# Two products of the third projection placed together behind the first products of each level

## The chip, the cores and the metric

The kernel runs on one core of one Trainium2 chip. The metric is the device time in microseconds (us) of one execution; the median of the runs shown counts.

## The reference, cut to what matters

Two transformer blocks over 512 tokens of width 1024. The change lies in the second block, in its RWKV-7 mixer. Sixteen heads of 64 columns each keep a 64x64 state that is updated token by token:

```python
def step(state, inp):
    r_t, w_t, k_t, v_t, a_t, b_t = inp
    sa = jnp.einsum('bhij,bhj->bhi', state, a_t)
    state = state * w_t[:, :, None, :] + sa[..., None] * b_t[:, :, None, :] + v_t[..., None] * k_t[:, :, None, :]
    return state, jnp.einsum('bhij,bhj->bhi', state, r_t)
```

The inputs r, k and v of a pair of heads are three projections of the normed tokens, `proj = n @ w_in`, 128 columns each. The dilated attention beside it reads projections of the same tokens.

## The kernel before, in words

The kernel is one program with the engines' instruction streams written out by hand: each engine has its own block of code, and they meet only through counted semaphores. `p_pe.step("p10")` on an instruction means that it raises TensorE's counter when it is done; `pe.wait_ge(p_dve.sem, p_dve.done("z10", at))` holds TensorE's stream until VectorE has done the step of that name.

**The mixer's passes.** The RWKV heads are worked on in eight passes, one pair of heads each. `pair_pass` stands once in each engine's block (TensorE line 1752, ScalarE 2545, VectorE 3307; GpSimd's part is `level_masks`, line 1185). TensorE runs passes 0 to 6 with `ahead=True` and the eighth, the last, with `ahead=False`. Time is cut into 8 chunks of 64 tokens, and the recurrence inside the chunks is written as a triangular matrix (the transition matrix), which is inverted by block doubling.

**The levels.** After the 2x2 blocks, which are made directly, five levels (`LEVELS = (2, 4, 8, 16, 32)`, counted l = 0 to 4 in the code, one to five in the title) double the size of the blocks. A level for the halves e = 0 and 1 of a pair is this chain:

- GpSimd masks the part of the matrix that belongs to the level into `MT` (line 1193, steps m{l}{e}).
- TensorE multiplies it with `XZ[..., 0, ...]` into banks 0 and 1, the level's first products (line 1846, steps p{l}{e}, 16 matmuls of 64x64 for each e; in level l = 1 line 1848 adds as many products of another use between them).
- ScalarE copies the result from PSUM to `PM` (line 2573, steps pm{l}{e}).
- TensorE multiplies `PM` with `XZ`, the level's second products, 32 matmuls (lines 1868 and 1870, steps xz{l}{e}; in the last level line 1870 alone, 16 matmuls).
- VectorE adds them to `XZ` (line 3334, steps z{l}{e}). The next level's first products for e wait for z{l}{e}; behind the last level the products of line 1879 wait for z41.

Between levels VectorE also mixes and scales the next pair's inputs (lines 3239 to 3245, after levels l = 0 and 1). Behind the last level it does the next pair's key norm (lines 3250, 3252, 3254), then line 3346, then line 3350, which needs TensorE's line 1897 and for which the scan over the chunks (from line 1932 on) waits. Behind the levels TensorE has line 1879, the gate products (lines 1884 and 1885), line 1897 and further products.

**The filling work.** A projection of the next pair is 24 matmuls into bank 7: for each of the 8 tiles k of the inner dimension three matmuls of 128x128 weights with 512 columns (high by high, low by high, high by low part; `split_fill`, lines 1725 to 1727). TensorE issues them in pieces between the steps of the chain:

- projection 0 of the next pair (r) as a whole at the beginning of the pass;
- projection 1 (k) with tiles 0 to 4 before level l = 0, and 5 to 7 inside it;
- projection 2 (v), the third, called `early`, one tile behind the first products and one behind the second products of each of the levels l = 1 to 4: tiles 2l-2 and 2l-1. In the last pass `early` is instead a projection of the dilated attention, with the same tiles at the same places.

```python
                    if l:
                        early(range(2 * l - 2, 2 * l - 1))
                    ...
                        mm.then_inc(p_pe.sem, p_pe.step(f"xz{l}{e}"))
                    if l:
                        early(range(2 * l - 1, 2 * l))
```

In level l = 3 a product for the key norm follows (line 1856, not in the last pass), in l = 4 the one of line 1860. When tile 7 is done, `freed` lets SyncE load the slot of the weights anew, and ScalarE copies bank 7 away (line 2498, step raw2). SyncE issues the weights' loads in a fixed order (lines 1044 to 1065); ScalarE makes their high part (line 2469) and GpSimd their low part (line 1169).

Of the kernel before, what the change touches and what calls it, by code (L numbers as in the profile page):

```python
# [311 lines left out]
def two_blocks(nc, a, consts_d, bias_d, out):  # L312

    ctx = ExitStack()
    with ctx:
# [925 lines left out]
        def _(pe):  # L1241
# [510 lines left out]
            def pair_pass(i, at, p_pe, p_act, p_dve, p_pool, ahead):  # L1752

                if ahead:
                    early = lambda ks: projection(2, ks, "raw1", "A", "lv")
                    late = lambda ks: dilated(i, ks, "gg", "B", "ld")
                else:
                    early = lambda ks: dilated(7, ks, "dila", "B", "l7")
                    late = lambda ks: dilated(8, ks, "gg", "A", "l8")

                def projection(u, ks, read, buf, low):

                    s = ring.slot("rw", u)
                    if ks[0] == 0:
                        if u:
                            pe.wait_ge(p_act.sem, p_act.done(read, at))
                            pe.wait_ge(p_pool.sem, p_pool.done(low, at))
                        else:
                            pe.wait_ge(rw_act.sem, rw_act.before("dil", i))
                            if i:  # L1770
                                pe.wait_ge(rw_pool.sem, rw_pool.done("lr", i - 1))
                            else:
                                pe.wait_ge(rf_pool.sem, rf_pool.done("l1"))
                    mm = split_fill(s, buf, ks, bank[7])
                    if ks[-1] == KD - 1:
                        mm.then_inc(freed[s], 1)

                def dilated(u, ks, read, buf, low):

                    if ks[0] == 0:  # L1780
                        pe.wait_ge(p_act.sem, p_act.done(read, at))
                        pe.wait_ge(p_pool.sem, p_pool.done(low, at))
                    mm = split_fill(None, buf, ks, bank[7])
                    if ks[-1] == KD - 1:
                        mm.then_inc(dw_used, 1)
# [52 lines left out]
                for l in levels:  # L1838
                    for e in range(2):
                        pe.wait_ge(p_pool.sem, p_pool.done(f"m{l}{e}", at))  # L1840
                        pe.wait_ge(p_dve.sem, p_dve.done(f"z{l - 1}{e}" if l else "xi", at))
                        for t in range(NT):
                            n = 4 * e + t
                            for c, own in enumerate(halves):
                                far = halves[1 - c]
                                mm = nc.tensor.matmul(bank[e][own, t * CHUNK:(t + 1) * CHUNK], MT[far, n, :], XZ[far, e, 0, t, :], start=True, stop=True)  # L1846
                                if l == 1:
                                    mm = nc.tensor.matmul(bank[6][own, n * HEAD:(n + 1) * HEAD], GR[own, n, 2, :], TOK[own, t, 3, halves[e]], start=True, stop=True)
                        mm.then_inc(p_pe.sem, p_pe.step(f"p{l}{e}"))
                    if l == 0 and ahead:  # L1850
                        projection(1, range(5, KD), "raw0", "B", "lk")
                    if l:
                        early(range(2 * l - 2, 2 * l - 1))
                    if l == 3 and ahead:
                        pe.wait_ge(p_act.sem, p_act.done("ksq", at))
                        nc.tensor.matmul(bank[6], PAIR_ONES, YS, start=True, stop=True).then_inc(p_pe.sem, p_pe.step("kss"))
                    if l == 4:
                        pe.wait_ge(p_act.sem, p_act.done("kroot" if ahead else "akv", at))
                        pe.wait_ge(p_dve.sem, p_dve.done("rk", at))
                        nc.tensor.matmul(bank[6], PAIR_ONES, RK, start=True, stop=True).then_inc(p_pe.sem, p_pe.step("bonus"))  # L1860
                    for e in range(2):
                        pe.wait_ge(p_act.sem, p_act.done(f"pm{l}{e}", at))
                        pe.wait_ge(p_dve.sem, p_dve.done(f"z{l - 1}{e}" if l else "zi", at))
                        for t in range(NT):
                            n, cols = 4 * e + t, slice(t * CHUNK, (t + 1) * CHUNK)
                            for c, own in enumerate(halves):
                                if l < len(LEVELS) - 1:
                                    nc.tensor.matmul(bank[2 + 2 * e][halves[1 - c], cols], XZ[own, e, 1, t, :], PM[own, n, :], start=True, stop=True)
                            for own in halves:
                                mm = nc.tensor.matmul(bank[3 + 2 * e][own, cols], PM[own, n, :], XZ[own, e, 1, t, :], start=True, stop=True)  # L1870
                        mm.then_inc(p_pe.sem, p_pe.step(f"xz{l}{e}"))
                    if l:
                        early(range(2 * l - 1, 2 * l))
                pe.wait_ge(p_act.sem, p_act.done("akv", at))
                pe.wait_ge(p_dve.sem, p_dve.done(f"z{len(LEVELS) - 1}1", at))
                for n, (e, t) in enumerate(items):
# [83 lines left out]
            for i in range(RW_PAIRS - 1):  # L1960
                pair_pass(i, i, rw_pe, rw_act, rw_dve, rw_pool, True)
            pair_pass(RW_PAIRS - 1, 0, rz_pe, rz_act, rz_dve, rz_pool, False)

            pe.wait_ge(rz_act.sem, rz_act.done("groot"))
# [272 lines left out]
            early = range(KD - 1)  # L2237
# [1342 lines left out]
```

## Time and profile before

| what | value |
|---|---|
| median of 3 runs | 2744.73 us (2743.4 to 2746.04) |
| time of the profiled execution | 2746.42 us |
| its span, first to last instruction | 2744.6 us |
| TensorE matmuls busy | 2641.0 us, 96% of the span |
| VectorE busy | 1686.4 us, 61% |
| ScalarE busy | 702.7 us, 26% |
| GpSimd busy | 325.9 us, 12% |
| mean granted TensorE clock | 0.988 |

The profiled execution took 1.8 us more than its span, and 1.69 us more than the median. Engines in the rows: PE is TensorE's matmul, PEld its weight load, DVE VectorE, ACT ScalarE, POOL GpSimd, SPq SyncE's DMA queue. All weights and temporaries of the mixer lie in the tiles named W, RWF, HXB and ARENA. Matmul ends are modelled and overlap the next start, so the starts are what to read.

### The profile page before, as it was taken

What the parts mean: (1) busy time and instruction counts of PE and PEld (TensorE: products, weight loads), DVE (VectorE), ACT (ScalarE), POOL (GpSimd) and SP (SyncE); (2) the same over time, 40 slices, a digit from 0 to 9 for tenths busy, and PEclk for the clock granted to TensorE, in tenths of its full rate; (3) what the DMA queues carried; (4) which work ended last, traced back from release to release, by engine and by line L of the source; (5) the groups of instructions that cost most, each with busy time, mean ns of one, the idle gap of its engine ahead of it and who ended that gap; (6) DMA issues with size and microseconds to landing.
All of it is one profiled execution on the core that took longest, in us unless ns stands there. A gap on an engine that the chain in (4) does not pass through costs nothing.

```text
span 2744.6 us, 43636 instructions
## 1 busy us (share of the span) xinstructions
PE 2641.0 (96%) x17855; PEld 1988.4 (72%) x17855; DVE 1686.4 (61%) x2208; ACT 702.7 (26%) x1213; POOL 325.9 (12%) x282
## 2 busy tenths in 40 slices
PE   7999899999999999999989999989999999999998
PEld 4545556888878878888667677766577887788887
DVE  4888766555466665554567777663554666755554
ACT  4234433111010121110243444333431211211102
POOL 2000321000000000000232333322010000100001
PEclk9999999999999999999999999999999999999999
DMA  7675203333323323323311111122133333233332
GB/s 267 195 249 191 80 24 100 98 93 96 96 85 100 92 84 99 99 88 100 100 36 45 54 39 35 35 66 77 37 105 90 94 116 100 70 98 94 100 93 75
DMA packets 394845, 260.29 MB, mean 95 GB/s; under 512 B 19831, under 2 KB 376784, under 8 KB 394320
## 3 DMA queue, kind: packets, MB, share of 16 engines
q1 hardware_dynamic: 391456, 246.78, 30.0%
q0 software_dynamic: 2768, 9.83, 1.1%
q8 instruction: 108, 1.77, 0.3%
q10 hardware_dynamic: 480, 1.64, 0.1%
q14 instruction: 33, 0.27, 0.0%
HBM read 252.96 MB, written 4.46 MB: 94 GB/s over the span
## 4 chain that ended last, share of the span: by engine, by line
PE 83%; DVE 12%; issue 2%; ACT 2%; DMA 1%; DVEq 0%; SPq 0%; POOL 0%; ACTq 0%
PE PS L899 15%; PE PS L901 15%; PE PS L900 15%; PE PS L914 3%; PE PS L916 3%; PE PS L915 3%; PE PS L1725 3%; PE PS L1727 2%; PE PS L1726 2%; DVE ARENA L2812 2%; PE PS L1846 1%; PE PS L886 1%; PE PS L1439 1%; PE PS L1974 1%; PE PS L1619 1%
## 5 line engine op out<-in xcount | busy, mean ns | idle before, releaser
L925 DVE CAST WH<-W 128x1024 fp32r<-128x1024 f32 (+1 forms) x304 | 211.6, 696 | 419.3 <-PE PS L901 375.7
L927 DVE TENSOR_TENSOR WL<-W,WH 128x1024 fp32r<-128x1024 f32 (+1 forms) x304 | 371.1, 1221 | 10.4
L900 PE MATMUL PS<-XNL,WH 128*128 128x512 f32 x960 | 373.5, 389 | 0.0
L899 PE MATMUL PS<-HH,WH 128*128 128x512 f32 x672 | 262.0, 390 | 0.2 <-DVE HL L3197 0.2
L900 PE MATMUL PS<-HL,WH 128*128 128x512 f32 x672 | 261.5, 389 | 0.0
L901 PE MATMUL PS<-HH,WL 128*128 128x512 f32 x672 | 261.4, 389 | 0.0
L899 PE MATMUL PS<-XNH,WH 128*128 128x512 f32 x640 | 249.9, 391 | 11.5 <-DVE ARENA L3437 11.5
L901 PE MATMUL PS<-XNH,WL 128*128 128x512 f32 x640 | 249.0, 389 | 0.0
L900 PEld LDWEIGHTS PS<-XNL,WH 128*128 128x128 f32 x960 | 180.2, 188 | 37.7 <-issue 0.7
L914 PE MATMUL PS<-XNH,WH 128*128 128x512 f32 x384 | 151.1, 393 | 0.6 <-DVE XNL L845 0.5
L916 PE MATMUL PS<-XNH,WL 128*128 128x512 f32 x384 | 149.5, 389 | 0.0
L915 PE MATMUL PS<-XNL,WH 128*128 128x512 f32 x384 | 149.4, 389 | 0.0
L899 PEld LDWEIGHTS PS<-XNH,WH 128*128 128x128 f32 x640 | 120.1, 188 | 39.7 <-DVE WL L927 14.5
L899 PEld LDWEIGHTS PS<-HH,WH 128*128 128x128 f32 x672 | 126.1, 188 | 28.1 <-DVE HL L3547 1.3
L807 POOL TENSOR_TENSOR HXF<-HXF 128x512 f32<-128x512 f32 x24 | 36.8, 1532 | 916.0 <-ACT HXF L798 916.0
L901 PEld LDWEIGHTS PS<-HH,WL 128*128 128x128 f32 x672 | 126.1, 188 | 26.1
L900 PEld LDWEIGHTS PS<-HL,WH 128*128 128x128 f32 x672 | 126.1, 188 | 26.0
L901 PEld LDWEIGHTS PS<-XNH,WL 128*128 128x128 f32 x640 | 120.1, 188 | 25.0
L1727 PE MATMUL PS<-XNH,RWF 128*128 128x512 f32 x336 | 134.2, 400 | 0.0
L899 PE MATMUL PS<-XN2H,WH 128*128 128x512 f32 x320 | 126.5, 395 | 0.0
L1725 PE MATMUL PS<-XNH,RWF 128*128 128x512 f32 x260 | 121.9, 469 | 4.8 <-POOL RWF L1169 4.1
L901 PE MATMUL PS<-XN2H,WL 128*128 128x512 f32 x320 | 124.6, 389 | 0.0
(546 smaller groups left out, 4955.8 us busy)
## 6 DMA issues: line engine op xcount, KB each, us to landing
ARENA<-in_ada_w SPq DMA_DIRECT2D x80, 512.0 KB, 5.1
W<-in_ffn_w SPq DMA_DIRECT2D x64, 512.0 KB, 3.8
W<-in_w_in SPq DMA_DIRECT2D x51, 512.0 KB, 3.8
W<-in_ffn_w_gate SPq DMA_DIRECT2D x44, 512.0 KB, 3.6
W<-in_ffn_w_up SPq DMA_DIRECT2D x44, 512.0 KB, 3.6
W<-in_ffn_w_down SPq DMA_DIRECT2D x32, 512.0 KB, 3.9
W<-in_sc_w_in SPq DMA_DIRECT2D x24, 512.0 KB, 3.7
ARENA<-in_ada_w SPq DMA_DIRECT2D x8, 1024.0 KB, 18.5
```

Source lines behind the costliest of these rows:

```text
L899: nc.tensor.matmul(dst, WH[:, h, c], hi(k), start=(start and k == 0), stop=False)
L900: nc.tensor.matmul(dst, WH[:, h, c], lo(k), start=False, stop=False)
L901: mm = nc.tensor.matmul(dst, WL[:, h, c], hi(k), start=False, stop=(stop and k == kts - 1))
L914: nc.tensor.matmul(dst[u], WH[:, h, c], hi(k), start=(k == 0), stop=False)
L915: nc.tensor.matmul(dst[u], WH[:, h, c], lo(k), start=False, stop=False)
L916: mm = nc.tensor.matmul(dst[u], WL[:, h, c], hi(k), start=False, stop=(k == KD - 1))
L925: nc.vector.tensor_copy(WH[:, h, 0:n], W[:, s, 0:n]).then_inc(parted, 1)
L927: nc.vector.tensor_tensor(WL[:, h, 0:n], W[:, s, 0:n], WH[:, h, 0:n], ALU.subtract).then_inc(freed[s], 1)
L1725: nc.tensor.matmul(dst, high[:, c], XNH[:, k, :], start=(k == 0), stop=False)
L1726: nc.tensor.matmul(dst, high[:, c], XNL[:, k, :], start=False, stop=False)
L1727: mm = nc.tensor.matmul(dst, low[:, h, c], XNH[:, k, :], start=False, stop=(k == KD - 1))
L2812: nc.vector.scalar_tensor_tensor(ACC[:, b % 2, :], AW[:, u, :], SILU_C[:, k, 0:1], ACC[:, b % 2, :], ALU.mult, ALU.add).then_inc(aw_used[u ...
```

## The change

It is two lines in TensorE's stream. In each of the levels l = 1 to 4 (two to five) both tiles of `early` are issued behind the first products; nothing of it stands behind the second products any more. Level l = 0 and all other engines' code are as before, and the number of instructions is the same.

```diff
                     if l:
-                        early(range(2 * l - 2, 2 * l - 1))
+                        early(range(2 * l - 2, 2 * l))
                     if l == 3 and ahead:
...
                         mm.then_inc(p_pe.sem, p_pe.step(f"xz{l}{e}"))
-                    if l:
-                        early(range(2 * l - 1, 2 * l))
                 pe.wait_ge(p_act.sem, p_act.done("akv", at))
                 pe.wait_ge(p_dve.sem, p_dve.done(f"z{len(LEVELS) - 1}1", at))
```

## Rows read from the trace of the kernel before

**Rows 1.** The page: busy time by engine, and the chain that ended last.

```profile
PE 2641.0 (96%) x17855; PEld 1988.4 (72%) x17855; DVE 1686.4 (61%) x2208; ACT 702.7 (26%) x1213; POOL 325.9 (12%) x282
...
PE 83%; DVE 12%; issue 2%; ACT 2%; DMA 1%; DVEq 0%; SPq 0%; POOL 0%; ACTq 0%
```

**Rows 2.** Busy time by stretch: pass by pass, PEclk is the granted clock.

```profile
1453.00:1511.00 58.00, 55.56 (x1037) 41.51 (x1035) 41.51 (x56) 23.44 (x41) 18.73 (x16) 1.00 0.14 39
1511.00:1570.00 59.00, 57.15 (x1047) 42.74 (x1045) 41.73 (x59) 24.03 (x42) 18.92 (x17) 1.00 0.18 49
...
1686.00:1744.00 58.00, 56.07 (x1040) 41.71 (x1040) 41.58 (x58) 23.61 (x40) 18.74 (x16) 1.00 0.15 41
```

**Rows 3.** Timeline of level l = 2 in the third pass (start, duration, engine, line).

```profile
1542.53 0.30 PEld L1846 LDWEIGHTS PS<-ARENA 64*64 64x64 f32 x7 [0.36 <-issue]
...
1543.26 0.85 ACT L2573 ACTIVATE ARENA<-PS 128x256 f32<-128x256 f32 x2 [1.10 <-PE PS L1846]
1543.30 1.86 POOL L1193 TENSOR_TENSOR ARENA<-ARENA,CONST 128x256 f32<-128x256 f32 x2 [2.10 <-PE PS L1846]
...
1543.61 0.50 PE L1725 MATMUL PS<-XNH,RWF 128*128 128x512 f32 x1
...
1544.50 0.27 PE L1868 MATMUL PS<-ARENA 64*64 64x64 f32 x2
...
1545.35 1.28 DVE L3334 TENSOR_TENSOR ARENA<-ARENA,PS 128x512 f32<-128x512 f32 x2 [0.77 <-PE PS L1870]
...
1545.59 0.50 PE L1725 MATMUL PS<-XNH,RWF 128*128 128x512 f32 x1
...
1546.48 0.39 PE L1846 MATMUL PS<-ARENA 64*64 64x64 f32 x6
```

**Rows 4.** Chain of waits inside a run of fills: piece start, length.

```profile
1531.43 0.23 PE PS L1725
1531.65 0.23 PE PS L1726
1531.88 0.23 PE PS L1727
1532.11 0.23 PE PS L1725
```

**Rows 5.** Timeline, same pass: second products of l = 0 to first of l = 1.

```profile
1536.74 0.27 PE L1868 MATMUL PS<-ARENA 64*64 64x64 f32 x2
...
1537.60 1.28 DVE L3334 TENSOR_TENSOR ARENA<-ARENA,PS 128x512 f32<-128x512 f32 x2 [0.34 <-PE PS L1870]
...
1538.40 0.13 PEld L1846 LDWEIGHTS PS<-ARENA 64*64 64x64 f32 x1 [0.63 <-issue]
1538.43 0.24 PE L1846 MATMUL PS<-ARENA 64*64 64x64 f32 x1 [0.52 <-DVE ARENA L3334]
```

**Rows 6.** Timelines: the same gap in the first pass; additions of other passes.

```profile
1421.32 0.27 PE L1868 MATMUL PS<-ARENA 64*64 64x64 f32 x2
...
1422.88 0.13 PEld L1846 LDWEIGHTS PS<-ARENA 64*64 64x64 f32 x1 [0.54 <-issue]
...
1483.18 0.68 DVE L3334 TENSOR_TENSOR ARENA<-ARENA,PS 128x512 f32<-128x512 f32 x1
...
1599.38 1.28 DVE L3334 TENSOR_TENSOR ARENA<-ARENA,PS 128x512 f32<-128x512 f32 x2
1603.34 1.29 DVE L3334 TENSOR_TENSOR ARENA<-ARENA,PS 128x512 f32<-128x512 f32 x2 [0.78 <-PE PS L1870]
1608.14 1.28 DVE L3334 TENSOR_TENSOR ARENA<-ARENA,PS 128x512 f32<-128x512 f32 x2 [3.52 <-PE PS L1870]
```

**Rows 7.** Timeline, third pass: from the last level to the scan over chunks.

```profile
1554.12 0.27 PE L1870 MATMUL PS<-ARENA 64*64 64x64 f32 x2
...
1554.94 0.89 DVE L3334 TENSOR_TENSOR ARENA<-ARENA,PS 128x256 f32<-128x256 f32 x2 [3.49 <-PE PS L1870]
...
1556.09 1.96 PE L1879 MATMUL PS<-ARENA 64*64 64x128 f32 x32
1556.19 3.35 DVE L3252 RECIPROCAL RSTD<-RSTD 128x512 f32<-128x512 f32 x1
...
1560.09 0.69 PE L1897 MATMUL PS<-ARENA 64*64 64x64 f32 x32
...
1561.00 1.40 DVE L3350 TENSOR_TENSOR ARENA<-PS,CONST 64x512 f32<-64x512 f32 x2
```

**Rows 8.** Timeline of the last pass: where TensorE waits for ScalarE instead.

```profile
1848.64 0.69 PE L1897 MATMUL PS<-ARENA 64*64 64x64 f32 x32 [0.60 <-ACT ARENA L2595]
```

**Rows 9.** The last pass: weight loads after idle time, a fill, busy time (PE, PEclk).

```profile
1821.84 1.81 PEld L1846 LDWEIGHTS PS<-ARENA 64*64 64x64 f32 x32 [3.05 <-POOL ARENA L1193]
1827.16 0.13 PEld L1846 LDWEIGHTS PS<-ARENA 64*64 64x64 f32 x1 [2.09 <-issue]
1830.21 0.18 PEld L1868 LDWEIGHTS PS<-ARENA 64*64 64x64 f32 x2 [0.65 <-ACT ARENA L2584]
...
1828.64 0.79 PE L1725 MATMUL PS<-XNH,HXB 128*128 128x512 f32 x1
...
1827.00:1830.40 3.40, 3.21 (x75) 0.66 0.00 0
```

**Rows 10.** Timeline: weights for the next pass, and their first use.

```profile
1510.12 1.06 ACT L2469 ACTIVATE RWF<-W 128x1024 fp32r<-128x1024 f32 x1 [6.57 <-DMA W<-in_w_in]
...
1511.26 2.38 POOL L1169 TENSOR_TENSOR RWF<-W,RWF 128x1024 fp32r<-128x1024 f32 x1 [17.36 <-ACT RWF L2469]
...
1519.15 0.19 PEld L1725 LDWEIGHTS PS<-XNH,RWF 128*128 128x128 f32 x1 [0.24 <-ACT ARENA L2538]
```

## The prediction

> **What bounds the kernel now.** The page comes first: TensorE's matmuls are busy for 96% of the span, and the chain that ended last lies on PE for 83% and on DVE for 12% [rows 1]. So time is lost where TensorE stands still, or where VectorE carries the chain. Next the stretches: a steady pass of the mixer takes 58 to 59 us at a granted clock of 1.00, with PE busy for 56 to 57 of them [rows 2]. Then the timeline of one level shows what holds it together [rows 3]. The level l = 2 begins with its first products at 1542.53. One tile of fill starts at 1543.61, the second products at 1544.50, the other tile at 1545.59, the next level at 1546.48. That is 1.08 + 0.89 + 1.09 + 0.89 = 3.95 us in which TensorE always has something to issue. Each tile covers one round trip: the first the copies by ScalarE, the second the additions by VectorE. The question is how long each trip is without its tile.
>
> **The trip to ScalarE.** Its two copies stand from 1543.26 to 1544.11 [rows 3], while TensorE would be free for the second products at about 1543.6. The first copy is half of 0.85 us and done at about 1543.68, the second at 1544.11, when the 16 second products of e = 0 (half of 1.09 us) would be about through. One tile covers this fully; a second tile covers nothing more.
>
> **The trip to VectorE.** From the first of the second products to the first addition it is 0.85 us [rows 3]. One addition takes 0.68 us [rows 6], and the second starts 0.60 us behind the first (1.28 - 0.68). The next level's first products may begin after the first addition. What this gap is with no tile in it, the kernel shows already, between l = 0 and l = 1, where nothing stands: from 1536.74 to 1538.40, 1.66 us, with 0.52 us of PE idle put down to the addition [rows 5]. The addition ends at 1538.28, so the hand-over costs 0.12 us. This is the nearest row to the new state, and I take its price, 1.65 us, for all levels.
>
> On that hand-over there is a rule. The weight load of the waiting product starts 0.12 us after the addition's end and its matmul 0.03 us later [rows 5]; the load didn't run ahead. The Trainium skill (TensorE: Matmul & The Clock Gate, "Step-by-step: what each phase is for") says that TensorE pulls weight loads ahead of running matmuls; by it the load could be over when the addition ends, which would give back some 0.03 us in each of 24 levels, under 1 us. The row goes against that where a semaphore is awaited, and I give nothing for it.
>
> **Each edit, step by step, per pass.**
> 1. The tile added behind the first products. In a run of fills a tile of three matmuls costs 0.68 us (1531.43 to 1532.11) [rows 4]; alone it costs 0.89 [rows 3], since 0.20 us go into the switch from and to the small products. As it joins a run, it costs 0.69 with the rounding. Bounds: 0.68 and 0.89.
> 2. The tile taken away behind the second products. Before, from second products to the next level: 1.98 us (1544.50 to 1546.48) [rows 3]. After: 1.65. That gives back 0.33 us, no more, since the chain takes over from the tile. Bounds for the gap: 1.56 from the first pass [rows 6], and as far above, 1.75; so 0.23 to 0.42 is given back.
> 3. The second half. After the wait TensorE needs 0.54 us for e = 0 and then finds the second addition: 1.65 + 0.54 = 2.19 us after the start of the second products, while that addition ends at 0.85 + 1.28 = 2.13 and is seen 0.12 later, at 2.25. A stall of some 0.06 us, for the first products of l = 2, 3, 4. Before, these had started late enough. Bounds: 0 and 0.12.
> 4. Levels l = 1, 2, 3 together: 3 x (0.69 - 0.33) + 3 x 0.06 = 1.26 us. The additions keep the same cadence in other passes (1599.38, 1603.34, 1608.14) [rows 6], so one level stands for all.
> 5. The last level. Its second products start 0.69 us later by the tile ahead of them. Before, the additions ended at 1555.83 and line 1879 started at 1556.09, 1.97 us after 1554.12 [rows 7]; without a tile it can start at 1.71 + 0.12 = 1.83 us. For TensorE the loss is 0.69 - 0.14 = 0.55 us. But VectorE is behind it: after the additions it has the key norm with a reciprocal of 3.35 us, and reaches line 3350 at 1561.00, when line 1897 has been over since about 1560.78 [rows 7]. So the path goes through VectorE, and it is the additions' shift, 0.69, that counts.
> 6. Sum of a pass: 1.26 + 0.69 = 1.95 us. In the last pass there is no key norm, TensorE's line 1897 waits for ScalarE behind line 1879 instead [rows 8], and the loss is 1.26 + 0.55 = 1.81.
>
> What else is moved? The tiles issue no DMA. Weights of the third projection are freed a little earlier; no load waits on that, since SyncE's loads for the next pass stand behind the gate's. GpSimd's masks for the next level are done at 1545.16, 2.63 us after the level's start [rows 3], and would be needed some 4.3 us after it: free. Nothing is queued behind TensorE's new wait but its own stream; VectorE and ScalarE wait for that stream, and so the loss passes on in full. What covers the chain from now on is only the two tiles and, in l = 3 and 4, the products of lines 1856 and 1860, all on the side that needs no more cover.
>
> Seven passes at 1.95 and one at 1.81: 13.65 + 1.81 = 15.5 us. Against the profiled execution: 2746.42 + 15.5 = 2761.9. That execution stands 1.69 us above the median, so the median comes to 2760.2 us, 0.56% more. With all bounds at one end a pass costs 3 x (0.68 - 0.42) + 0.68 = 1.5 us, at the other 3 x (0.89 - 0.23 + 0.12) + 0.89 = 3.2: sums of 12 and 26 us. The high end needs the lone tile's price for a tile in a run, which rows 4 speak against; I take 22 as the far end.
>
> **Rivals.** A change of under 0.2% (5.5 us) can't be told from none by a measurement of this kernel.
> - *Absorbed.* Some wait of the pass doesn't move with TensorE and takes the loss in. The candidate is the weights' landing: ScalarE idles 6.57 us for it [rows 10]. But their low part is ready at about 1513.6 and TensorE first reads it at 1519.15, held by a copy. So 5 us of slack, and the loads follow the gate products anyway. It would give 2745 to 2750; chance 0.06.
> - *Half of it.* The loss shows in the levels, but is made up partly behind them, where TensorE idles before the scan for VectorE. Half of 15.5 gives 2752.5; chance 0.08.
> - *Not slower, the wait isn't met.* Place: the end of the second products in l = 1 to 4. If the sum of second products and hand-over were under 1.09 us, no wait would replace the tile, and each level would save one switch of 0.20 us: 32 x 0.20 = 6.4 us, giving 2738.3. It decides at an addition ending within 1.1 us of the first second product; it ends at 1.53 [rows 3, 6]. Chance 0.03.
> - *The clock falls.* TensorE now idles about 0.5 us at each level's end. In the last pass the granted clock was 0.66 in the stretch from 1827.0, a mix of its levels of 2.4 and 1.2 GHz, behind idle times of 3.05 and 2.09 us [rows 9]. At the lower clock a tile took 1.57 us there instead of 0.89 (1828.64 to 1830.21). The Trainium skill (TensorE: Matmul & The Clock Gate, "HAM oscillation — how this bites in real kernels") warns of just this: idle gaps between bursts of matmuls put the clock back to half. One level of each pass at 1.2 GHz would cost some 2 us: 8 x 2 = 16 us more, 2776. The gap at l = 0, as long as the new ones, left the clock at 1.00 in every steady pass [rows 2, 5]. Chance 0.05.
>
> **How the numbers follow.** The forecast has 0.78. Its own range is 2756 to 2767, from 12 us and 22 us on the same base (2746.42 - 1.69). To hold 8 in 10 with the half case at its edge I give 2752 to 2768, which leaves out the absorbed, the faster and the clock case, 0.14. The absorbed case is the one within 0.2%. Faster by over 0.2%: 0.03; within: 0.06; slower: 0.91.
>
> **What would show it.** Right: six fills in a row behind the first products; 1.57 us from fill to second products in l = 1 and 2; 1.65 from second products to the next level, with PE idle of 0.4 to 0.6 us put down to line 3334, 24 times, and before line 1879 8 times; level l = 2 at about 4.4 us instead of 3.95; steady passes near 60 us; clock still 1.00 there. Wrong: a gap of under 1.3 us behind the second products, or levels as computed but passes still at 58 us; then step 2 or step 5 falls. Passes with granted clocks under 1.00 speak for the last rival.

## The result and the profile after

The change makes the kernel slower. The median is 2760.9 us (2759.14 to 2763.53, 4 runs) against 2744.75 us before: the ratio is 1.006, with an interval of 1.0047 to 1.0073. A second set of runs gave 1.0068 (1.0053 to 1.0084). In the set of the first four experiments below, two executions of the kernel before and one of `behind1` fell into a much slower state (3612, 5309 and 4419 us); the ratios leave them out. The span grew from 2744.6 to 2760.1 us, by 15.5. In the profile after, all lines behind the change stand two lower: 3334 is 3332, 3350 is 3348, 1879 is 1877, 1897 is 1895.

The head of the page and the chain hardly tell the two kernels apart; TensorE's busy time is what it was [rows 1]:

```profile
span 2760.1 us, 43636 instructions
...
PE 2641.2 (96%) x17855; PEld 1995.2 (72%) x17855; DVE 1683.1 (61%) x2208; ACT 702.4 (25%) x1213; POOL 326.9 (12%) x282
```

From the first addition of the second pass to that of the seventh, a pass took 57.6 us on average before (1479.37 to 1767.40) and takes 59.25 after (1483.09 to 1779.34). The stretches, laid along the passes, show less PE busy in 59 and 60 us than before in 58 and 59, and the clock still at 1.00, its level of 2.4 GHz [rows 2]. Columns: stretch, length, then busy time of PE, PEld, DVE, ACT, POOL, the granted clock, DMA share and GB/s.

```profile
1457.00:1516.00 59.00, 54.85 (x1035) 41.95 (x1034) 40.79 (x55) 23.40 (x41) 19.14 (x17) 1.00 0.14 38
1516.00:1576.00 60.00, 55.92 (x1044) 43.02 (x1042) 40.61 (x57) 24.82 (x42) 20.16 (x17) 1.00 0.16 46
```

The timeline of level l = 2 in the third pass answers to rows 3:

```profile
1546.72 1.28 DVE L3332 TENSOR_TENSOR ARENA<-ARENA,PS 128x512 f32<-128x512 f32 x2 [0.61 <-PE PS L1870]
...
1547.52 1.17 PEld L1846 LDWEIGHTS PS<-ARENA 64*64 64x64 f32 x32 [0.63 <-issue]
1547.55 1.28 PE L1846 MATMUL PS<-ARENA 64*64 64x64 f32 x32 [0.52 <-DVE ARENA L3332]
...
1548.76 0.50 PE L1725 MATMUL PS<-XNH,RWF 128*128 128x512 f32 x1
...
1550.34 0.27 PE L1868 MATMUL PS<-ARENA 64*64 64x64 f32 x2
...
1551.20 1.29 DVE L3332 TENSOR_TENSOR ARENA<-ARENA,PS 128x512 f32<-128x512 f32 x2 [1.45 <-PE PS L1870]
...
1552.00 0.30 PEld L1846 LDWEIGHTS PS<-ARENA 64*64 64x64 f32 x7 [0.63 <-issue]
```

Read the starts. Level to level it is 1547.52 to 1552.00, 4.48 us, where it was 3.95. The two tiles take 1.58 us (1548.76 to 1550.34); from the second products to the next level it is 1.66 us (1550.34 to 1552.00). The PE idle put down to the addition is 0.52 us at the start of the level shown. And the first products themselves last 1.24 us up to the first fill (1547.52 to 1548.76) instead of 1.08 (1542.53 to 1543.61 [rows 3]): their 32 weight loads are spread over 1.17 us, where they took 1.01 before. The first row below is the load with which the second half, e = 1, begins in the changed kernel. It comes 0.60 us after the first load and 0.12 us after the end of the second addition (1546.72 + 1.28 = 1548.00). The second row has the loads of the kernel before:

```profile
1548.12 0.13 PEld L1846 LDWEIGHTS PS<-ARENA 64*64 64x64 f32 x1
```

```profile
1542.53 1.01 PEld L1846 LDWEIGHTS PS<-ARENA 64*64 64x64 f32 x32 [0.36 <-issue]
```

The list of who waited for whom shows the same once for all: TensorE waited for the additions 5.6 us in 8 places before, and does so after the change in 32 places, plus 8 at line 1877, where there was no such entry:

```profile
PE PS L1846 <- DVE ARENA L3332: 18.6, 32, 3.0
...
PE PS L1877 <- DVE ARENA L3332: 5.5, 8, 0.7
```

Behind the last level (to be held against rows 7), line 3348 comes 1567.91 - 1561.85 = 6.06 us after the first addition; before it was 1561.00 - 1554.94 = 6.06 as well:

```profile
1561.03 1.15 PE L1870 MATMUL PS<-ARENA 64*64 64x64 f32 x32
1561.85 0.89 DVE L3332 TENSOR_TENSOR ARENA<-ARENA,PS 128x256 f32<-128x256 f32 x2 [4.02 <-PE PS L1870]
...
1562.88 1.96 PE L1877 MATMUL PS<-ARENA 64*64 64x128 f32 x32 [0.70 <-DVE ARENA L3332]
1563.11 3.35 DVE L3250 RECIPROCAL RSTD<-RSTD 128x512 f32<-128x512 f32 x1
...
1566.88 0.69 PE L1895 MATMUL PS<-ARENA 64*64 64x64 f32 x32
...
1567.91 0.67 DVE L3348 TENSOR_TENSOR ARENA<-PS,CONST 64x512 f32<-64x512 f32 x1
```

A good ruler for all kernels below is VectorE's cadence, that is, the starts of the first addition in each level, and of line 3350 behind them. For the fourth pass (before: 1595.57, 1599.38, 1603.34, 1608.14, 1612.92, 1618.99) the steps are, in us:

| kernel | l 0 to 1 | 1 to 2 | 2 to 3 | 3 to 4 | 4 to line 3350 | sum |
|---|---|---|---|---|---|---|
| before | 3.81 | 3.96 | 4.80 | 4.78 | 6.07 | 23.42 |
| after | 4.50 | 4.48 | 5.34 | 5.31 | 6.08 | 25.71 |
| l5_only | 3.82 | 3.94 | 4.81 | 5.47 | 6.07 | 24.11 |
| l2_4_only | 4.50 | 4.49 | 5.34 | 4.61 | 6.07 | 25.01 |
| behind1 | 4.29 | 4.25 | 5.11 | 5.06 | 6.07 | 24.78 |
| behind2 | 4.03 | 4.02 | 4.89 | 4.85 | 6.06 | 23.85 |
| mirror | 3.82 | 3.28 | 4.57 | 4.77 | 6.61 | 23.05 |
| mirror45 | 3.83 | 3.93 | 4.12 | 4.78 | 6.61 | 23.27 |
| norm_early | 4.50 | 4.48 | 5.34 | 5.32 | 5.79 | 25.43 |
| l0_tile | 4.23 | 3.79 | 4.81 | 4.78 | 6.07 | 23.68 |
| cover_where_none | 4.50 | 4.42 | 4.65 | 4.78 | 5.92 | 24.27 |

### The profile page after: what moved, and what is told of

Read it like the earlier page. It is cut to its first block, busy times and chain, and to the rows that moved or that the text cites. A ratio compares the mean times of both kernels' runs of the same rounds, so it can differ in the third digit from the quotient of the medians.

```text
span 2760.1 us, 43636 instructions
## 1 busy us (share of the span) xinstructions
PE 2641.2 (96%) x17855; PEld 1995.2 (72%) x17855; DVE 1683.1 (61%) x2208; ACT 702.4 (25%) x1213; POOL 326.9 (12%) x282
## 4 chain that ended last, share of the span: by engine, by line
PE 84%; DVE 11%; issue 2%; ACT 2%; DMA 1%; DVEq 0%; SPq 0%; POOL 0%; ACTq 0%
PE PS L899 15%; PE PS L901 15%; PE PS L900 15%; PE PS L914 3%; PE PS L916 3%; PE PS L915 3%; PE PS L1725 3%; PE PS L1727 2%; PE PS L1726 2%; DVE ARENA L2810 2%; PE PS L1846 2%; PE PS L886 1%; PE PS L1533 1%; PE PS L1439 1%; PE PS L1972 1%
```

## The experiments

Each ratio below is against the kernel before timed in the same set. Its median was 2745.26 us beside `l5_only`, `l2_4_only`, `behind1` and `behind2`; 2745.81 beside `mirror`, `mirror45`, `norm_early` and `l0_tile`; 2745.72 beside `cover_where_none`, `code_shifted` and the change again; and 2747.04 beside `code_shifted_timed`. "My theory" and "rival" stand for what I wrote down before each run.

**One part alone.** The two places of the change were made apart. `l5_only` and `l2_4_only`:

```diff
-                        early(range(2 * l - 2, 2 * l - 1))
+                        early(range(2 * l - 2, 2 * l if l == 4 else 2 * l - 1))
...
-                    if l:
+                    if l and l < 4:
                         early(range(2 * l - 1, 2 * l))
```

> Only in level l = 4 do both tiles stand behind the first products; l = 1 to 3 are as before. My theory: the tile ahead of the last second products puts them off by 0.69 us, VectorE's key norm hands that on in full, so line 3350 stays 6.06 us behind the last level's first addition and a steady pass costs 0.69 us, the last one 0.55: 5.4 us in all, 2750 us. Rival (the path runs through TensorE there): only 0.55 us a pass, 4.4 us in all, and line 3350 comes 0.14 us closer to the addition. Rival (the loss sits in the waits of the lower levels alone): under 1 us.

Measured: 2750.78 us against 2745.26, ratio 1.0021 (1.0011 to 1.0031). The step into the last level grew from 4.78 to 5.47 us, by 0.69, and line 3350 stayed 6.07 us behind: VectorE hands the delay on in full. Of the two rivals the second falls by the time; the first, whose time is too near, falls by the cadence.

> Both tiles behind the first products in l = 1 to 3 only, l = 4 as before. My theory: from first addition to first addition 4.50 us instead of 3.81, 4.48 instead of 3.94, 5.34 instead of 4.81, and 4.61 instead of 4.78 in the last level; 1.59 us a pass, 12.7 us in all, 2757 us. Rival (a run of six fills is itself slower, waits are harmless): the fills of the run would start more than 0.23 us apart, and no PE idle would be put down to the additions.

Measured: 2756.34 us, ratio 1.0042 (1.0018 to 1.0066). The cadence is 4.50, 4.49, 5.34, 4.61, as written down. The waits for the additions are 17.7 us in 32 places, where they were 5.6 in 8: in each pass three new ones stand beside the one behind l = 0, which was there before. The rival fails on both of its signs: the fills of a run start 0.23 to 0.24 us apart behind the first (1605.74, 1605.97, 1606.21, 1606.44, 1606.67 in the fourth pass), as in the long runs [rows 4], and PE idle is put down to the additions. The time is the least sharp here, with 1.0018 to 1.0066. The two parts together cost 24.11 - 23.42 + 25.01 - 23.42 = 2.28 us a pass, the whole change 2.29: they add up.

**The dose.** If a wait of fixed length is what costs, a few matmuls left in the gap should already fill it. Here a level keeps one or two of the six matmuls behind the second products (`behind1`; `behind2` has `(0,)` and `(1, 2)` in place of `(0, 1)` and `(2,)`; `split_fill` got an argument that says which of a tile's three matmuls it issues):

```diff
                         early(range(2 * l - 2, 2 * l - 1))
+                        early(range(2 * l - 1, 2 * l), (0, 1))
...
-                        early(range(2 * l - 1, 2 * l))
+                        early(range(2 * l - 1, 2 * l), (2,))
```

> In l = 1 to 4 one of the six matmuls stands behind the second products, five ahead of them. My theory (the chain sets the gap at 1.65 us as long as what stands in it is shorter): second products plus one fill are 1.09 + 0.43 = 1.52 us, so the gap stays 1.65 us and the fill in it is free; a pass costs 0.46 + 3 x (0.46 - 0.33 + 0.16) = 1.33 us, 10.5 us in all, 2755 us. Rival (loss in proportion to the matmuls moved): two thirds of the change's 16 us, 10.8 us, and the gap grows to 1.75 us or more.

> In l = 1 to 4 two of the six matmuls stand behind the second products, four ahead. My theory: the two fills with their switch (0.66 us) are as long as the wait, the gap is 1.75 us and no idle is put down to the additions; a pass costs 0.23 us (in the last level) and nothing in the others, 1.7 us in all, 2746.5 us. Rival (loss in proportion to the matmuls moved): one third of the change's 16 us, 5.4 us, 2750 us.

Measured: 2753.64 us (1.0029, 1.0014 to 1.0044) and 2746.29 us (1.0005, 0.9995 to 1.0015). With one matmul behind, three levels lose 0.28 to 0.31 us and the first 0.48, 1.36 a pass where 1.33 was expected. The gap stays as long as it is with nothing in it: in the fourth pass it is 1.69 us from the first of the second products to the next first product (1601.40 to 1603.09), and as much between l = 0 and l = 1, where no matmul stands (1597.12 to 1598.81). With two, the waits for the additions are 5.4 us in 8 places, about what they were before (5.6):

```profile
PE PS L1849 <- DVE ARENA L3338: 5.4, 8, 1.8
```

Line 1849 is line 1846 there. A pass still costs 0.43 us more, 0.06 to 0.09 in the later levels, twice what was expected. A loss in proportion to the matmuls moved would come to much the same for `behind1`, but to 5.4 us, a ratio of 1.0020, for `behind2`; that lies outside its interval.

**The opposite order.** `mirror` puts both tiles behind the second products in all four levels, `mirror45` in l = 3 and 4 only:

```diff
-                    if l:
-                        early(range(2 * l - 2, 2 * l - 1))
...
-                        early(range(2 * l - 1, 2 * l))
+                        early(range(2 * l - 2, 2 * l))
```

> The opposite of the change: in l = 1 to 4 both tiles stand behind the second products, none behind the first. My theory: ScalarE's copies take about 0.1 us more than the first products cover, and one switch of 0.2 us between the kinds of products goes away, so l = 1 and 2 gain about 0.1 to 0.2 us each; in l = 3 and 4 the products of lines 1856 and 1860 cover the copies, so l = 3 gains 0.12, and in l = 4 the last additions end 0.8 us earlier, which takes VectorE off the path and leaves TensorE on it: 0.7 us a pass, 5.5 us in all, 2739.5 us. Rival (each side needs its own tile; the copies' trip is as long as the additions'): the wait for the copies costs as much as the change's wait did, 0.4 us or more a level, 2755 us or more. Rival (the order does not matter once the number of tiles is the same): 2745 us.

> Both tiles behind the second products in l = 3 and 4 only, where other products cover the copies; l = 1 and 2 as before. My theory: 0.12 us gained in l = 3, and line 3350 of VectorE now waits for TensorE, 0.39 us a pass earlier than before: 3 us in all, 2742 us, and about 3 us above the kernel with all four levels so. Rival (copies not covered): slower than before.

Measured: 2745.09 us (1.0001, 0.9991 to 1.0011) and 2744.37 us (0.9999, 0.9989 to 1.0008). That the copies' trip needs a tile of its own is refuted: leaving it without one costs nothing that can be measured, while leaving the additions' trip bare costs 16 us. (In l = 3 and 4 the products of lines 1856 and 1860 still stand there, so only l = 1 and 2 are bare.) But the gain I expected isn't there either. The fourth pass is 0.37 us shorter in `mirror` and 0.15 in `mirror45`, about half of what I wrote or less: what the levels gain is partly paid back behind the last one, where line 3350 comes 6.61 us after the addition instead of 6.07, now waiting for TensorE. And in `mirror` three passes of the first seven, the second, third and seventh, need 24.4 to 24.7 us, 1.0 to 1.3 more than the 23.42 of the table and together 4.6 more than three passes of 23.05. In the third the two additions of l = 2 are torn apart, 1544.72 and 1545.82, while in the fourth they follow each other within 1.29 us:

```profile
1540.98 1.27 DVE L3332 TENSOR_TENSOR ARENA<-ARENA,PS 128x512 f32<-128x512 f32 x2
1544.72 0.69 DVE L3332 TENSOR_TENSOR ARENA<-ARENA,PS 128x512 f32<-128x512 f32 x1 [0.97 <-PE PS L1868]
1545.82 0.69 DVE L3332 TENSOR_TENSOR ARENA<-ARENA,PS 128x512 f32<-128x512 f32 x1 [0.41 <-PE PS L1868]
...
1602.13 1.29 DVE L3332 TENSOR_TENSOR ARENA<-ARENA,PS 128x512 f32<-128x512 f32 x2 [0.21 <-DVE ARENA L3239]
```

TensorE idles there in the midst of the second products, in l = 1 and in l = 2, for no engine that the trace names. (In the second and the seventh pass it idles so for 1.33 and 1.34 us, up to 1482.96 and 1770.48.)

```profile
1540.37 0.13 PEld L1868 LDWEIGHTS PS<-ARENA 64*64 64x64 f32 x1 [0.62 <-issue]
...
1545.25 0.13 PEld L1868 LDWEIGHTS PS<-ARENA 64*64 64x64 f32 x2 [0.48 <-issue]
```

**VectorE behind the last level.** `norm_early` is the changed kernel with the maximum and the reciprocal of the key norm (lines 3252 and 3254 there) ahead of the last additions:

```diff
+                    if l == 3 and ahead:
+                        key_inverse(at, p_act, p_dve)
                 if ahead:
-                    key_norm(at, p_act, p_dve)
+                    key_normed(at, p_dve)
```

> The changed kernel with VectorE's maximum and reciprocal of the key norm moved ahead of the last level's additions, where VectorE idles 4.0 us. My theory (behind the last level the path runs through VectorE by about 0.3 us): line 3350 comes 5.79 us behind the first addition of the last level instead of 6.06, a steady pass is 0.27 us shorter, 1.9 us in all, 2759 us. Rival (TensorE alone sets the path there): line 3350 stays at 6.06 us. Rival (the reciprocal now delays the last additions): more than 5.34 us between the first additions of l = 3 and l = 4.

```profile
1557.96 3.35 DVE L3254 RECIPROCAL RSTD<-RSTD 128x512 f32<-128x512 f32 x1
1561.62 0.89 DVE L3339 TENSOR_TENSOR ARENA<-ARENA,PS 128x256 f32<-128x256 f32 x2 [0.30 <-PE PS L1870]
...
1567.42 0.68 DVE L3357 TENSOR_TENSOR ARENA<-PS,CONST 64x512 f32<-64x512 f32 x1 [3.49 <-PE PS L1895]
```

The last line is what matters: the operation now waits for TensorE's line 1895 and comes 5.80 us behind the addition, not 6.06. So in the changed kernel VectorE set the path there, by 0.27 us a pass. The time, 2759.96 us with a ratio of 1.0056 (1.0039 to 1.0073), can't be told from the change's 1.006.

**A tile where none stood.** The gap between l = 0 and l = 1 has no cover [rows 5]. `l0_tile` puts the second projection's last tile there:

```diff
-                        projection(1, range(5, KD), "raw0", "B", "lk")
+                        projection(1, range(5, KD - 1), "raw0", "B", "lk")
...
                         mm.then_inc(p_pe.sem, p_pe.step(f"xz{l}{e}"))
+                    if l == 0 and ahead:
+                        projection(1, range(KD - 1, KD), "raw0", "B", "lk")
```

Left out of the cut is ScalarE's side: its step hd, the next weights' high part, goes behind the copies of l = 1.

> The kernel before with a tile put where none stands: the last tile of the second projection goes from behind the first products of l = 0 to behind its second products, and ScalarE's high part of the next weights goes behind l = 1, so that it doesn't delay the copies. My theory (a tile behind the second products costs only 0.33 us where nothing stood, and saves 0.69 in front): 0.36 us a pass gained, 2.6 us in all, 2742 us. Rival (VectorE's mixing, which now gets its input 0.4 to 0.7 us later, delays the additions of l = 1): no gain, and more than 3.81 us from the additions of l = 0 to those of l = 1 by more than TensorE saves.

Measured: 2744.13 us, 0.9998 (0.9988 to 1.0007): no difference that shows. The third pass explains both halves of it. The additions of l = 0 start right behind another operation of VectorE, with no idle time ahead, where they had waited 0.34 us for TensorE before: TensorE is ready earlier, but VectorE isn't. And the rival holds. The mixing behind them (line 3241 there) idles 0.33 us for ScalarE's copy of the projection, which waits for the moved tile, and the additions of l = 1 stand right behind the mixing, 4.24 us after those of l = 0 instead of 3.81. The next step makes up only 0.17 of that.

```profile
1536.34 0.74 DVE L3282 SCALAR_TENSOR_TENSOR ARENA<-ARENA,COLS 128x512 f32<-128x512 f32 x1
1537.00 1.27 DVE L3336 TENSOR_TENSOR ARENA<-ARENA,PS 128x512 f32<-128x512 f32 x2
1538.60 0.69 DVE L3241 TENSOR_TENSOR ARENA<-ARENA 128x512 f32<-128x512 f32 x1 [0.33 <-ACT ARENA L2500]
...
1541.24 1.27 DVE L3336 TENSOR_TENSOR ARENA<-ARENA,PS 128x512 f32<-128x512 f32 x2
```

`cover_where_none` moved VectorE's operation ahead of the additions (step rk) as well, behind the additions of l = 1, and the key norm's maximum ahead of the last level's additions:

> Built on the kernel before and on the l0_tile kernel: the last tile of the second projection covers the additions of l = 0, line 3280's product (step rk) goes from ahead of these additions to behind those of l = 1, and the key norm's maximum goes ahead of the last level's additions. My theory: the additions of l = 0 start 0.69 us earlier (in the l0_tile kernel VectorE's step rk had held them), 0.42 us a pass gained there, and 0.14 us behind the last level, where line 3350 then waits for TensorE: 0.56 us a pass, 3.9 us in all, 0.14% less than before. Rival (VectorE is full there: the moved step delays the additions of l = 2): no gain.

Measured: 2747.23 us, 1.0003 (0.9994 to 1.0012). My theory fell, the rival stood: VectorE's mixing (line 3243 there) now ends at 1547.6 and the additions of l = 2 start behind it at 1547.82 instead of behind TensorE. Only the last step, 5.92 instead of 6.07, came as expected. The levels were 0.85 us longer in the fourth pass, more than was gained ahead of them. In l = 1 the cause is that of `l0_tile`: the mixing idles 0.59 us for ScalarE's copy, and the additions start right behind it at 1543.40.

**TensorE's own code.** `code_shifted` is the kernel before with waits ahead of the passes that are long fulfilled. By the instruction counts of the two profiles (43700 and 43636) they became 64 instructions, so the shift was 64 places and not 128:

```diff
+            for _ in range(128):
+                pe.wait_ge(rf_act.sem, rf_act.done("ksq"))
             for i in range(RW_PAIRS - 1):
```

> The kernel before with 128 waits that are long fulfilled ahead of TensorE's passes: the same work, its instructions 128 places further on. In the kernel before the second and the seventh pass need 1.0 and 0.4 us more in l = 1 (4.92 and 4.39 us to the additions of l = 2 instead of 3.94), in idle time that the trace puts down to no engine, each soon after a packet of the instruction queue. My theory (TensorE waits for its own code there): the stalls move to other passes or other levels. Rival (the stall belongs to those passes' data, waits or transfers): the same two passes show it.

In the kernel before, the second pass has its two additions of l = 1 at 1483.18 and 1484.60; with the shift they follow each other, and the seventh pass is whole too (1768.53 to 1772.48, 3.95 us). First before, then shifted:

```profile
1483.18 0.68 DVE L3334 TENSOR_TENSOR ARENA<-ARENA,PS 128x512 f32<-128x512 f32 x1
1484.60 0.69 DVE L3334 TENSOR_TENSOR ARENA<-ARENA,PS 128x512 f32<-128x512 f32 x1 [0.73 <-PE PS L1870]
```

```profile
1482.79 1.28 DVE L3336 TENSOR_TENSOR ARENA<-ARENA,PS 128x512 f32<-128x512 f32 x2
...
1486.74 1.28 DVE L3336 TENSOR_TENSOR ARENA<-ARENA,PS 128x512 f32<-128x512 f32 x2 [0.77 <-PE PS L1870]
```

The stalls went by a shift that changes no work, so they don't belong to those passes' data. Pure chance is a poor account too: `l5_only` and `mirror45`, whose code up to there is as long as before, need 4.37 to 4.38 us in l = 1 of the same two passes, instead of 3.94. The stalls did not reappear in another pass's levels, which I had expected. The time was then measured:

> The kernel with its code shifted again, now timed. One look gave a span 4.4 us below the first one of the kernel before, 1.4 us of it from the two stalls in l = 1. My theory (stalls on TensorE's own code are worth 3 to 4 us in the kernel before): ratio about 0.9987, 2742 us, below both kernels. Rival (one look was a lucky execution): within 0.05% of the kernel before.

Measured: 2745.12 us, 0.9995 (0.9986 to 1.0005), with a span of 2740.3 us. The second to the seventh pass have again no such stall (23.41 to 23.42 us each), yet the times can't be told from before. It is the lowest ratio of all kernels here, and still not shown to beat the kernel before.

**The change again.**

> The changed kernel once more, beside the others: 0.5 to 0.6% above the kernel before, and again 25.70 us from the additions of l = 0 to line 3350 in the steady passes, with the second and the seventh showing no stall above that.

Measured: 2762.97 us, 1.0068, and 25.70 to 25.71 us in the second to the sixth pass. The seventh had 25.96, a stall of 0.26 us that the first profile had not shown; in that point the expectation was missed.

## Why the prediction was right

I gave 2760.2 us and 2760.9 was measured, with the sign and the range right. The steps one by one:

- *Step 1, the tile ahead:* 0.69 us. In `l5_only`, where it stands alone, it is 0.69. Right.
- *Step 2, the gap:* 1.65 us by the row between l = 0 and l = 1. After: 1.66. `behind1` shows the mechanism: a matmul in the gap is free, and the gap stays 1.69 us by the starts of the products, as long as the chain is longer. Right.
- *Step 3, the second half:* this is the mis-sized term. I had 0.06 us with a bound of 0.12; the first products need 1.24 us up to the first fill instead of 1.08, so 0.16, outside my bound. The wait itself was read rightly: I had put the second half's start 2.25 us after the second products, and it came at 1548.12, 2.25 us after those of that level (1545.87). What was wrong is the 0.54 us for e = 0. I had halved the 1.08, which holds the switch to the fill too; sixteen of the 32 weight loads take (1.01 - 0.14) / 31 x 16 = 0.45 us by the row of the kernel before, so TensorE is ready at 2.10 and stands 0.15. A level costs 0.69 - 0.33 + 0.16 = 0.52 us, not 0.42, and with three such stalls a pass this makes 0.3 us.
- *Step 5, the last level:* the tile's 0.69 us passed on in full through VectorE (`l5_only`), and `norm_early` shows it is VectorE by 0.27 us. By the table a pass costs 0.69 + 0.52 + 0.54 + 0.53 = 2.28 us in its first four steps and nothing in the fifth; I had 1.95.
- *The last pass:* from the additions of l = 0 (1839.97) to line 3348 (1864.57) 24.60 us against 23.03, so 1.57 where I had 1.81. This is not a firm figure: in the second profile of the same kernel, `after_again`, it is 23.34 us. The whole difference lies in the first step, 5.66 and 4.40 us, and goes with the clock: in the first profile the granted clock was 0.57 from 1840.0 to 1844.0, inside that step; in the second it was 0.70 from 1834.0 to 1839.6, ahead of it, and 1.00 from there on.

So the levels lost more than forecast: summed over the eight passes, from the first additions of l = 0 to line 3350, 15.95 us. That is near the forecast of 15.5 mainly because two passes of the kernel before had stalls of 0.97 and 0.45 us in l = 1. The changed kernel has no stall above its waits there. Six steady passes at 2.29 would have lost 13.7 us; they lost 12.3 (the second 1.31, the seventh 1.84). Outside the levels the two profiles differ too: 1.8 us more ahead of the first pass's levels, 2.6 less between the passes, 0.3 more behind. I had no term for these, and with them the sum is the 15.5 of the spans. Nothing ties them to the change: over all profiles here the time between the levels of the passes lies between 235.0 and 239.1 us, with the kernel before (239.1) at the top and the changed kernel at 236.6 and 237.2. That my sum came out at the same number is therefore partly luck. A term too small by 0.34 us a pass, 2.4 us in seven, was met by 1.4 us of stalls in the kernel before, by 0.24 us each in the first pass (it lost 2.05) and the last, and by the 0.5 us outside the levels. The medians lie 16.15 us apart in the first set and 17.25 in the second, a little above the spans' 15.5.

The rivals: the loss wasn't absorbed, nor made up by half, since line 3350 stays at its distance. The wait was met in all levels, so the faster case was wrong. The clock held 1.00 in the steady passes, with idle times of 0.52 us, so the clock rival was wrong too. What the Trainium skill describes (TensorE: Matmul & The Clock Gate, "HAM oscillation — how this bites in real kernels") is a kernel whose bursts of matmuls are parted by waits for DMA several times as long, so these gaps don't contradict it; I had read it too widely when I wrote that it warns of just this.

## What to carry to other kernels

Independent work that is strewn into a chain of dependent steps should be laid out by the length of each trip, and that length can often be read at a place of the same kernel where nothing covers it. Here one side of a level left 1.65 - 1.09 = 0.56 us open, which two matmuls with their switch (0.66) cover, and the other next to none. Moving a tile from the side with the long trip to the other cost 0.52 us a level, about as much as the wait that was uncovered, while the opposite move cost nothing that could be measured. When a step is moved, follow it onto the other engines: a delay on TensorE came out through VectorE's chain, and a gain ahead was eaten by VectorE's own queue.

## What I had not expected of the hardware

TensorE stalls now and then with no engine as the releaser, and some of the places come back in several kernels: 0.48 and 0.62 us in the third pass of `mirror`, and 0.79 us in the second pass of the kernel before:

```profile
1484.01 0.14 PEld L1870 LDWEIGHTS PS<-ARENA 64*64 64x64 f32 x2 [0.79 <-issue]
```

In the cases looked at a packet of the instruction queue moved two to three us earlier: at 1481.7 us in the kernel before, with the stall ending at 1484.0, and between 1537 and 1538 in `mirror`, ending at 1540.37. By itself this says little, since the kernel before has some sixty such packets between 1420 and 1860 us, and most are followed by no stall. Shifting the code by 64 instructions removed both stalls of the kernel before from its levels. The place in the code doesn't settle it alone: of the two profiles of the changed kernel only the second has a stall in the seventh pass, and the one in the second pass is 0.97 us in the kernel before and 0.43 in `l5_only`. All this points to TensorE waiting for its own code, above all where many small products follow each other without long ones between; that the stall is the fetch itself was not shown, and how much such stalls are worth over the whole kernel stays open, since the shifted kernel's times don't differ beyond the interval.
